# Softmax scaling on ScalarE, and later sums for the modulation, in a fused transformer kernel

## The reference

```python
m_lat = (silu_c @ ada_w[i] + ada_b[i])[:, None, :]           # six vectors of 1024 per layer
sh_m, sc_m, g_m, sh_f, sc_f, g_f = jnp.split(m_lat, N_MOD, axis=-1)
h_lat = modulate(x, norm_mix_g[i], sh_m, sc_m)
# mla_mixer: low-rank queries, keys and values, rmsnorm of each head's q and k, rotary part
s = jnp.einsum('bqhd,bkhd->bhqk', qi, k, preferred_element_type=jnp.float32) * scale
p = jax.nn.softmax(s, axis=-1)
return jnp.einsum('bhqk,bkhd->bqhd', p.astype(v.dtype), v)
```

## Time and profile before

| | us |
|---|---|
| median of 3 runs | 971.33 (970.02 to 973.52) |
| the profiled execution | 973.88 |
| its span in the trace | 972.1 |
| PE busy in the span | 931.8 (96%) |
| DVE busy | 707.8 (73%) |
| ACT busy | 534.5 (55%) |
| POOL busy | 306.1 (31%) |

### The profile page before, as it was taken

The page is one execution under the profiler, slowest core; times in us unless marked ns, Lnnn a source line. Parts: engine busy times, 40 slices in busy tenths (PEclk is TensorE's granted clock), DMA queues, the critical chain, the costliest instruction groups (busy, mean ns, idle before and its releaser), DMA issues.

```text
span 972.1 us, 19442 instructions
## 1 busy us (share of the span) xinstructions
PE 931.8 (96%) x6866; PEld 868.9 (89%) x6866; DVE 707.8 (73%) x1134; ACT 534.5 (55%) x914; POOL 306.1 (31%) x272
## 2 busy tenths in 40 slices
PE   5988989899999999999979999999999999999996
PEld 5977557799999999988969999999999878999996
DVE  3998679779888777898886698655555774485764
ACT  3465655566665444555634566654444762574644
POOL 1952020128886011120051188740110000430012
PEclk9799989999999999999979999999999998899999
DMA  8856185167888777789647976556556423255421
GB/s 333 301 199 219 44 236 172 49 239 237 301 275 270 278 288 269 246 295 331 233 105 179 288 273 214 188 180 192 175 178 202 133 92 105 87 174 195 152 87 44
DMA packets 57268, 195.90 MB, mean 202 GB/s; under 512 B 6407, under 2 KB 10007, under 8 KB 56952
## 3 DMA queue, kind: packets, MB, share of 16 engines
q1 hardware_dynamic: 55528, 192.66, 59.4%
q0 software_dynamic: 1680, 2.44, 1.1%
HBM read 192.59 MB, written 1.44 MB: 200 GB/s over the span
## 4 chain that ended last, share of the span: by engine, by line
PE 82%; DVE 12%; issue 3%; ACT 2%; DMA 1%; POOL 0%; SPq 0%; DVEq 0%; ACTq 0%
PE bank L534 24%; PE bank L535 24%; PE bank L536 23%; DVE w_lo L1568 2%; DVE ada_raw L1575 1%; DVE products L1670 1%; PE bank L632 1%; PE bank L923 1%; PE bank L949 1%; DVE ada_raw L1670 1%; DMA x<-x_in 1%; PE bank L798 1%; DVE ada_more L1670 1%; PE bank L877 1%; DVE ada_raw L1583 1%
## 5 line engine op out<-in xcount | busy, mean ns | idle before, releaser
L1568 DVE TENSOR_TENSOR w_lo<-raw,w_hi 128x1024 fp32r<-128x1024 f32 (+1 forms) x261 | 338.2, 1297 | 92.6 <-ACT w_hi L1142 89.6
L1142 ACT ACTIVATE w_hi<-raw 128x1024 fp32r<-128x1024 f32 (+1 forms) x261 | 272.5, 1045 | 175.8 <-PE bank L536 167.3
L534 PE MATMUL bank<-act_hi,w_hi 128*128 128x258 f32 (+1 forms) x872 | 249.0, 286 | 0.0
L535 PE MATMUL bank<-act_lo,w_hi 128*128 128x258 f32 (+1 forms) x872 | 246.7, 283 | 0.0
L536 PE MATMUL bank<-act_hi,w_lo 128*128 128x258 f32 (+1 forms) x872 | 246.5, 283 | 0.0
L534 PEld LDWEIGHTS bank<-act_hi,w_hi 128*128 128x128 f32 x872 | 166.0, 190 | 2.4 <-issue 1.9
L535 PEld LDWEIGHTS bank<-act_lo,w_hi 128*128 128x128 f32 x872 | 166.1, 190 | 0.1
L536 PEld LDWEIGHTS bank<-act_hi,w_lo 128*128 128x128 f32 x872 | 166.2, 191 | 0.0
L534 PE MATMUL bank<-hid_hi,w_hi 128*128 128x256 f32 x512 | 143.9, 281 | 0.0
L535 PE MATMUL bank<-hid_lo,w_hi 128*128 128x256 f32 x512 | 143.9, 281 | 0.0
L536 PE MATMUL bank<-hid_hi,w_lo 128*128 128x256 f32 x512 | 143.9, 281 | 0.0
(11 more groups left out here) (353 smaller groups left out, 1809.8 us busy)
## 6 DMA issues: line engine op xcount, KB each, us to landing
raw<-weights SPq DMA_DIRECT2D x247, 512.0 KB, 3.9
ada_raw<-ada SPq DMA_DIRECT2D x88, 512.0 KB, 5.0
raw<-weights SPq DMA_DIRECT2D x14, 384.0 KB, 4.3
ada_more<-ada SPq DMA_DIRECT2D x8, 512.0 KB, 5.9
bias<-bias_by_distance SPq DMA_DIRECT2D x8, 256.0 KB, 6.8
x<-x_in SPq DMA_DIRECT2D x1, 1024.0 KB, 7.4
ctx<-ctx_in SPq DMA_DIRECT2D x1, 1024.0 KB, 9.4
out<-result SPq DMA_DIRECT2D x4, 256.0 KB, 2.7
```

What stands on the lines that cost most here:

```text
L534: pe.matmul(dst, w[0], a[0], start=start, stop=False)
L535: pe.matmul(dst, w[0], a[1], start=False, stop=False)
L1142: act.activation(w_hi[:, slot, 0:width_of(c)], raw[:, slot, 0:width_of(c)], ACT.Copy).then_inc(weight_hi, 1)
L1568: dve.tensor_tensor(w_lo[:, slot, 0:w], raw[:, slot, 0:w], w_hi[:, slot, 0:w].bitcast(fp32), ALU.subtract).then_inc(weight_lo, 1)
```

## The change

ScalarE takes the multiplication of the probabilities from VectorE. VectorE keeps the reciprocal (`inverse_sum`), which now comes behind the modulate of its own step rather than behind the next step's logits. Modulates 3 to 7 leave their places between query parts and norms and stand in one block ahead of the attention loop; in the loop step u has modulate 7 + u from u = 1 to 14, and modulates 22 and 23 come behind the last two output copies. On SP, weight chunks 19 to 23 are requested ahead of modulation chunk 7.

```diff
@@ SP
-            for a in range(4, ADA_EARLY):
-                if 12 + a < 26:
-                    load_weights(12 + a)
+            for a in range(4, 7):
+                load_weights(12 + a)
                 load_ada(a)
+            for c in range(19, 24):
+                load_weights(c)
+            for a in range(7, ADA_EARLY):
+                load_ada(a)
+                if a < 9:
+                    load_weights(17 + a)
@@ ACT, attention loop
-                act.wait_ge(latent.negmax, u + 1)
+                act.wait_ge(latent.negmax, 2 * u + 1)
...
-                for v in ([u - 1] if u > 0 else []) + ([u] if u == 2 * H - 1 else []):
+                for v in (u - 1, u):
+                    if v == u:
+                        act.wait_ge(latent.negmax, 2 * u + 2)
+                        act.activation(p_mla[:, u % 2, :], p_mla[:, u % 2, :], ACT.Copy,
+                                       scale=small[:, 80 + u:81 + u]).then_inc(latent.normed, 1)
+                    if v < 0 or v == u < 2 * H - 1:
+                        continue
@@ DVE, queries
             query_low(4)
+            query_low(5)
             convert(15)
-            query_low(5)
-            modulate(3)
-            convert(16)
             query_low(6)
             query_low(7)
-            modulate(4)
+            convert(16)
             convert(17)
@@ DVE, keys and norms
-            modulate(5)
             convert(19)
...
-            modulate(6)
             dve.wait_ge(k_rstd_high, 1)
...
-            modulate(7)
             convert(20)
+            for a in range(3, 8):
+                modulate(a)
+
+            def inverse_sum(u):
+                dve.wait_ge(latent.probs, u + 1)
+                dve.reciprocal(small[:, 80 + u:81 + u], small[:, 64 + u:65 + u]).then_inc(latent.negmax, 1)
@@ DVE, attention loop
-                if 1 <= u <= 2 * H:
-                    normalise(latent, u - 1, p_mla[:, (u - 1) % 2, :])
-                if u < 2 * H:
                     if u == 0:
                         convert(21)
-                    modulate(8 + u)
+                    elif u < 2 * H - 1:
+                        modulate(7 + u)
+                    inverse_sum(u)
...
+                if u >= 2 * H and qt == 0:
+                    modulate(22 + h - H)
```

## The result

Runs beside each other on one chip, median us (lowest to highest, runs):

| | before | changed | ratio, 95% interval |
|---|---|---|---|
| with the prediction | 971.43 (970.02 to 973.52, 4) | 964.56 (964.18 to 965.97, 4) | 0.9917 [0.9893, 0.9941] |
| again (e7_after_again) | 974.38 (971.01 to 980.72, 15) | 964.57 (962.22 to 967.83, 6) | 0.9902 [0.9864, 0.9941] |

A forecast was written before the change was run, and what follows sets the result against it. PE was taken to lose time between 90 and 189 us waiting for DVE, with modulates queued ahead. Gains of 6.9 + 0.2 + 0.4 + 1.0 = 8.5 us from 971.33 gave 962.8 us, range 960.0 to 967.8.

The forecast's parts named there:

- The base: The median of the kernel before, 971.33 us, from which the forecast subtracted its summed gain of 8.5 us.
- Should come out at the end undiminished: After 200 us: PE is busy throughout to 480 us, so any time gained earlier reaches the end in full.
- Queries: Query parts to key projection: without modulate 3 ahead, it starts 3.8 us earlier, then held by POOL's latent splits.
- To the first transposes: Key norms, block of five modulates and first logits: 3.1 us more, 6.9 us in all up to step 0's transposes.
- Heads and tail: From first transposes to output projection: 0.2 us at head 0 to 1, 0.4 in the loop, 1.0 in the tail.
- More: Rival, chance 0.13: the clock stays up before step 0, head 0 to 1 wins 1.5 us or more, 960.5 us.
- the wait for chunk 9: Head 0 to 1: modulate 9 waits for its late chunk, delaying PE's transposes up to 1.8 us, covered if the clock falls.
- ACT paces the loop: Rival, chance 0.18: ScalarE's order of copies and multiplications makes a head take 6.4 us; 4.2 us won, 967.1 us.
- The ring starves the loop: Rival, chance 0.05: late modulation chunks stop each step's softmax, a head takes 7.25 us; 3.0 us slower, 974.3 us.
- Nothing of use: Rival, chance 0.04: POOL and a late chunk 7 take back the gains before the loop; about 1 us left, 970 us.

The follow-up runs named there:

- e7_after_again: The changed kernel measured once more, unchanged: 964.57 us beside 974.38 us of the kernel before, ratio 0.9902.
- e1_queries: Kernel before with only the last two query parts moved ahead of chunks 16 and 17, modulates 3 and 4 behind chunk 17: 967.72 us, ratio 0.9937.
- e4_sp_order: Changed kernel with weight chunk 25 requested later, behind modulation chunk 11: 962.71 us, ratio 0.9892.
- e5_twice: Changed kernel with two more ScalarE passes over 128x256 into an unused tile ahead of each multiplication of the probabilities: 970.39 us, one run.
- e3_act_scale: Kernel before with only the multiplication moved to ScalarE and the reciprocal behind its own step's modulate: 969.87 us, ratio 0.9974.
- e8_before_busy: Kernel before with matmuls that nothing reads ahead of three waits of TensorE: 969.74 us beside 974.38 us, ratio 0.9949.
- e9_mix_busy: Kernel with weight chunk 25 requested behind modulation chunk 11, plus 28 unread matmuls in the gMLP's mixing that missed the pauses: 968.09 us, ratio 0.9945.
- e6_gaps: Kernel with weight chunk 25 requested behind modulation chunk 11, plus modulates 3, 4 and 5 taken out of the block of five: 961.15 us, ratio 0.9867.
- e2_dve_scale: Changed kernel with the multiplication of the probabilities put back on VectorE, modulates and SP's list as changed: 967.46 us, ratio 0.9938.
- e12_mix_dose: Kernel with weight chunk 25 requested behind modulation chunk 11, plus 11 and 5 unread matmuls at two pauses of the gMLP's mixing: 959.77 us, ratio 0.9861.
- e10_sp_again: Second measurement of the changed kernel with weight chunk 25 requested behind modulation chunk 11: 962.67 us beside 973.09 us, ratio 0.9889.

## Why the prediction was right

**The base.** The sum of 8.5 us lies between the gains measured (6.9 and 9.8 us between medians); the number it was taken from was not well known. Against 971.33 us, the median of three runs, it gave 962.8. Over all 69 runs of before in the five comparisons the median is 973.5, and 80% lie between 970.2 and 976.8; 973.5 - 964.6 is 8.9 us. From its own profiled execution the forecast was 965.4, and the changed kernel's profiled execution took 965.97. Before scatters by the clock and by the pace that e7_after_again shows: over 65 timed runs of before, each with its mean granted clock, the span grows by 0.91 us for each us of lost clock.

**"Should come out at the end undiminished"** was the weak step. It rested on 200 to 480 us, and there it held: 10.6 us ahead at 189 us, 10.4 at 477 us (start-up included). Behind 480 us, of which I had read no row, 0.8 us went in the mixing and 1.7 us in the gMLP's output projection. Both stages take the shorter time again in e7_after_again, with the same code.

**Queries: 3.8 us forecast, 4.35 measured** (27.73 to 23.38). The wait fell to 0.50 us and the eight rotary matmuls ran at 1.00. What stood next was not POOL:

```profile
88.23 4.77 POOL L2135 TENSOR_TENSOR om_lo<-tile_f,om_hi 128x256 fp32r<-128x256 f32 x4 [23.04 <-ACT om_hi L1152]
```

Its four splits took 4.77 us, not 5.78, and ended at 93.0; PE's key projection started at 93.50, straight behind its rotary matmuls. I had kept the old length because two conversions stayed beside them. The Trainium skill (GPSIMD Engine Reference, "Key points") has GpSimd contended by VectorE instructions with two SBUF inputs. The trace agrees in sign: with the modulate gone and only conversions and low parts beside them, the splits are 1.0 us shorter; which of DVE's instructions cost how much, no run here separates.

**To the first transposes: 6.9 us forecast, 7.4 measured.** `k_rstd_lo` waits for ACT, as said, and PE idles 0.53 us (forecast 0.5):

```profile
121.44 0.68 DVE L1797 TENSOR_TENSOR k_rstd_lo<-rstd,k_rstd_hi 8x512 fp32r<-8x512 f32 x1 [0.86 <-ACT k_rstd_hi L1320]
...
124.08 1.27 DVE L1586 CUSTOM_DVE_ANT_0 ada_raw<-ada_raw,silu_row,vec 128x1024 f32<-128x1024 f32 x1
...
130.11 0.68 DVE L1827 CUSTOM_DVE_ANT_0 scaled<-bank,sq 128x512 f32<-128x512 f32 x1
```

The five modulates took 6.03 us (forecast 6.0) and the first logits start at 130.11 (131.2 expected). The multiplication on ACT was bounded by 0.68 from the earlier trace rows:

```profile
132.24 0.72 ACT L1333 ACTIVATE p_mla<-p_mla,small 128x512 f32<-128x512 f32 x1 [0.30 <-DVE small L1808]
```

**Heads and tail: 1.6 us forecast (0.2 + 0.4 + 1.0), 2.7 measured** (48.10 to 45.39 us from the first transposes to the output projection; 45.73 in the second trace). This is the term that was mis-sized, and by its first part. I expected about 2.1 us of idle time before the first transposes and let the clock fall behind it, as it had behind the 2.45 us of the earlier trace rows. PE's idle time came in two pieces, 0.85 and 0.73 us, and nothing fell, in either trace of the changed kernel. That the shorter wait is the reason is not shown: in e1_queries the clock stayed up behind 2.44 us. The rival "More" had this step right. Without the fall the wait for chunk 9 had no cover: 1.5 us, within the size said for it (up to 1.8), measured by e4_sp_order. In the tail PE waits 1.30 us where 1.3 was said, but the second wait stayed at 0.69 us where 0.4 was said. Before:

```profile
183.86 0.66 PE L789 MATMUL bank<-const,p_mla 128*128 128x128 f32 x4 [2.00 <-DVE p_mla L1805]
...
187.37 1.99 PE L798 MATMUL bank<-pt_mla,v_mla 128*128 128x256 f32 x8 [0.69 <-ACT pt_mla L1330]
```

So the tail gave 0.7 us and not 1.0, and the heads 2.0 us where 0.2 + 0.4 were forecast; without the fall the prediction had 1.5 + 0.4 for them.

**Where luck helped.** To the output projection the kernel gained 10.1 us in one trace and 9.7 in the other, not the 8.5 of the sum; that is nearer to the 9.8 that "More" comes to by its 1.5 us than to the forecast. The time came out near the forecast because 2.2 us were lost behind the output projection in the profiled execution (776.57 to 778.75 us), and because the runs of before that the sum was taken from were 2 us faster than before's median over all runs.

**The rivals.** "ACT paces the loop" fell: heads at 5.77 and 5.78 us with PE busy throughout, and e5_twice shows the room. The Trainium skill (ScalarE: Activation LUTs, "Rules for kernel authors") wants such a multiplication on VectorE. The trace agrees on the instruction, 0.72 against 0.49 us; in e3_act_scale the kernel is 3.0 us faster by the medians for breaking the rule (the interval just reaches no change), as DVE was the releaser and ACT had the room. "The ring starves the loop" stopped at the two waits of 0.47 and 1.30 us (2.21 us in e7_after_again). "Nothing of use" is refuted by e1_queries.

**How much is the clock?** Before loses 6.8 us of it in the edited part, the changed kernel none, in both traces. e8_before_busy shows by itself that such falls cost time and that filling the pauses takes them away: 2.9 us gained, up to 5.0 without its overruns. So some 3 to 5 of the 10.1 us, by this estimate, are work that no longer ran at half clock. The timed runs agree: an execution of before loses 25.3 us of clock in the median of 65, one of the changed kernel 20.7 in the median of 10, which is 4.6 us less. The forecast booked 1.8 us for the clock, at the rotary matmuls.

## What to carry to other kernels

A wait of TensorE costs twice where the granted clock falls behind it: read the clock of the stretch after the wait, and price a shortened wait with and without the fall. Where a pause can't be removed, matmuls that nothing reads, fewer than the pause is long, can pay for themselves (2.9 us here); too many cost more than the fall (e9_mix_busy). Read also what else stands ahead of an instruction that you make ready sooner: in e6_gaps it was a table load. And before a sum is subtracted from a median of three, see how far single runs scatter, and read a row of every stage that "nothing changes in".

## What the runs showed of the hardware

- Matmuls of 128x256 in an unbroken run at a granted clock of 1.00 have two paces, 95 or 91 in 32 us (43.6 or 45.3 us for the gMLP's output projection). A stage keeps its pace for tens of us, the same kernel shows either in different executions, and the latent output projection in front (21.97 to 22.90 us) varies too. What chooses was not found.
- The granted clock falls to 0.50 or 0.51, the lower level of 1.2 GHz. Between 90 and 190 us the 14 traces have 15 waits of PE of 1.4 us or longer; behind 8 of them the clock fell before PE's next wait, behind 7 it did not. Nearly the same wait goes either way: 2.45 us in before with a fall, 2.44 us in e1_queries without; 2.00 us in before without, 2.02 us in e2_dve_scale and 2.03 us in e8_before_busy with one. The wait of 0.50 us ahead of the last query sums had a fall behind it in 5 of 11 traces (at 93.0 us in e12_mix_dose, none in e10_sp_again, with the same code there). No fall came behind the other waits under 1.4 us. A long pause makes a fall likelier, but a long one does not bring it for certain and a short one does not exclude it.
- ACT loads a table ahead of the first exponential, 1.28 us in every trace of this part that was read (before, changed, e6_gaps, e12_mix_dose).
